# Entering the third block by halves of the sequence: four columns on half 0 ahead of the norms of half 1

## What is computed

```python
h = h + odd_mixer(...)                 # (attn * silu(z)) @ w_out + b_out: the "output product"
h = rms_norm(h, final_norm_g)          # end of the second block
y = rmsnorm(h, norm_w)                 # start of the third block
proj = y @ w_in                        # columns: S5 u, S5 z, SSD z, conv input (x, B, C), dt
xbc = silu(causal_depthwise_conv_3(conv input, width 4))
dt = softplus(dt + dt_bias); A = -exp(A_log)
# SSD over chunks of 128, in four groups of heads, then its gate and norm; S5 and the output products after it
```

## Time and profile before

| | us |
|---|---|
| median of 3 runs (3431.41 to 3432.23) | 3431.87 |
| the profiled execution, own time | 3430.53 |
| its span on the core | 3428.7 |
| TensorE busy | 3157.4 (92%) |
| VectorE busy | 1670.7 (49%) |
| ScalarE busy | 1118.2 (33%) |
| GpSimd busy | 952.0 (28%) |
| share of TensorE in the chain that ended last | 80% |
| mean granted TensorE clock | 0.961 |

### The profile page before, as it was taken

The page is one execution under the profiler, slowest core; times in us unless marked ns, Lnnn a source line. Parts: engine busy times, 40 slices in busy tenths (PEclk is TensorE's granted clock), DMA queues, the critical chain, the costliest instruction groups (busy, mean ns, idle before and its releaser), DMA issues.

```text
span 3428.7 us, 38027 instructions
## 1 busy us (share of the span) xinstructions
PE 3157.4 (92%) x15348; PEld 2474.4 (72%) x15348; DVE 1670.7 (49%) x2730; ACT 1118.2 (33%) x1900; POOL 952.0 (28%) x699
## 2 busy tenths in 40 slices
PE   8999989999999999999999788599887788889998
PEld 6776667767788887778877556477665677778876
DVE  6979541012646543232424675377675234443425
ACT  2126451112521111133411754334343222232334
POOL 4210001113247772145212113011110122253422
PEclk9999999999999999999999899799998999999999
DMA  4110001113323332133311013211111233253222
GB/s 125 43 37 13 13 19 42 48 40 136 110 60 91 93 100 65 43 129 117 97 37 43 25 50 111 76 32 33 41 37 31 56 89 98 83 180 117 86 79 100
DMA packets 251055, 242.22 MB, mean 71 GB/s; under 512 B 15360, under 2 KB 198016, under 8 KB 249856
## 3 DMA queue, kind: packets, MB, share of 16 engines
q1 hardware_dynamic: 228944, 195.52, 18.8%
q10 hardware_dynamic: 21936, 44.27, 3.7%
HBM read 201.03 MB, written 38.73 MB: 70 GB/s over the span
## 4 chain that ended last, share of the span: by engine, by line
PE 80%; DVE 9%; ACT 5%; issue 2%; POOL 2%; DMA 1%; SPq 0%; ACTq 0%; DVEq 0%
PE psum L523 21%; PE psum L524 21%; PE psum L525 21%; PE psum L529 3%; PE psum L641 3%; PE psum L713 1%; PE psum L687 1%; DMA arena<-in_w_in 1%; PE psum L823 1%; PE psum L1116 1%; DVE arena L2783 1%; PE psum L1068 1%; POOL WS L2947 1%; PE psum L1067 1%; DVE arena L2567 1%
## 5 line engine op out<-in xcount | busy, mean ns | idle before, releaser
L2947 POOL TENSOR_TENSOR WS<-arena,WS 128x1024 fp32r<-128x1024 f32 x271 | 670.2, 2477 | 2008.5 <-ACT WS L1132 2008.1
L523 PE MATMUL psum<-XH,WS 128*128 128x512 f32 x2464 | 990.4, 402 | 27.4 <-POOL XL L3003 16.2
L524 PE MATMUL psum<-XL,WS 128*128 128x512 f32 x2464 | 968.4, 393 | 0.0
L525 PE MATMUL psum<-XH,WS 128*128 128x512 f32 x2464 | 967.8, 393 | 0.0
L523 PEld LDWEIGHTS psum<-XH,WS 128*128 128x128 f32 x2464 | 469.3, 190 | 140.2 <-issue 29.5
L524 PEld LDWEIGHTS psum<-XL,WS 128*128 128x128 f32 x2464 | 469.1, 190 | 98.2 <-issue 4.5
L525 PEld LDWEIGHTS psum<-XH,WS 128*128 128x128 f32 x2464 | 467.7, 190 | 100.0
L1132 ACT ACTIVATE WS<-arena 128x1024 fp32r<-128x1024 f32 x271 | 284.5, 1057 | 701.9 <-PE psum L525 243.8
L523 PE MATMUL psum<-WS,XH 128*128 128x512 f32 (+1 forms) x1024 | 396.3, 387 | 19.7 <-DVE XL L2005 7.1
L524 PE MATMUL psum<-WS,XH 128*128 128x512 f32 (+1 forms) x1024 | 393.2, 384 | 0.0
L525 PE MATMUL psum<-WS,XL 128*128 128x512 f32 (+1 forms) x1024 | 393.1, 384 | 0.0
(11 more groups left out here) (288 smaller groups left out, 3249.9 us busy)
## 6 DMA issues: line engine op xcount, KB each, us to landing
arena<-in_w_in SPq DMA_DIRECT2D x85, 512.0 KB, 3.9
arena<-in_w_out SPq DMA_DIRECT2D x48, 512.0 KB, 3.3
arena<-in_w_in_even SPq DMA_DIRECT2D x48, 512.0 KB, 4.1
arena<-in_w_out_even SPq DMA_DIRECT2D x32, 512.0 KB, 3.3
h_spill<-arena ACTq DMA_DIRECT2D x24, 512.0 KB, 3.1
arena<-s_table SPq DMA_DIRECT2D x8, 1536.0 KB, 6.8
arena<-in_w_in_odd SPq DMA_DIRECT2D x18, 512.0 KB, 3.8
s_table<-arena SPq DMA_DIRECT2D x32, 256.0 KB, 2.8
```

What stands on the lines that cost most here:

```text
L523: e.matmul(ps, wh, xh, start=start, stop=False)
L524: e.matmul(ps, wh, xl, start=False, stop=False)
L525: return e.matmul(ps, wl, xh, start=False, stop=stop)
L2947: e.tensor_tensor(lo, raw(book.raw_of.get(("w", u), 0), kbs, n), hi.bitcast(F32), SUB).then_inc(*w.up("w_lo", u))
```

## The change

TensorE's new order: product `ch` 0 (banks 0 to 3), two of the four pieces of product `ch` 1 (banks 4 to 7), the turn of half 0 (banks 0 to 3 again), the other two pieces, then `proj_first`: the dt column and the cv columns 0, 1, 2 of group 0 on half 0, the turn of half 1, the same four on half 1; dt's transposes, cv column 3, dt's small products; the first column of group 1 in both halves, and only then the chunks of group 0, woven as before with what is left.

On ACT the norms of half 1 are woven with these columns, two steps of `od_post(1)` and one copy out of PSUM. The Silus of group 0 come together after the last copy. `RAW3` gets two more buffers, in the room of the tiles of group 1, and the dt column is copied to `DTF`, in the room of `DD3`. The issue of ACT's constants and tables follows the turn of half 1. On DVE the additions of product `ch` 1 are woven one by one with the steps of `od_post(1)`; the convolutions of group 0 all come after the turn of half 1. On SP the weights of the five columns are issued ahead of the waits and the tables; POOL follows the same order of weights.

```diff
+        RAW3 += [view(at, 515) for at in (48.0625, 56.0625)]
+        DTF = [x.rearrange("p a b -> p (a b)") for x in DD3]
...
+        FIRST_RAW = [(0, 0), (1, 0), (2, 0), (0, 1), (1, 1), (2, 1), (3, 0), (3, 1)]
+
+        def ssd_order(prep, chunks, gate):
             for g in range(4):
                 other = chain(prep(g + 1) if g < 3 else iter(()), gate(g - 1) if g else iter(()))
+                if g == 0:
+                    for _ in range(2):
+                        next(other)
                 weave((chunks(g), 1, True), (other, 2 if g else 1, True))
...
(TensorE)
-            for ch in range(2):
-                run(proj_th("o3_ps", (ch,), w3, 512 * ch, 1, lambda tile: [("o3", ch, tile)], x="odo"))
-            for half in range(2):
-                turn_half("b3", XS3, half)
+            run(proj_th("o3_ps", (0,), w3, 0, 1, lambda tile: [("o3", 0, tile)], x="odo", ring=Banks(free_bank, [0, 1, 2, 3])))
+            o3_late = proj_th("o3_ps", (1,), w3, 512, 1, lambda tile: [("o3", 1, tile)], x="odo",
+                              ring=Banks(free_bank, [4, 5, 6, 7]))
+            for _ in range(2):
+                next(o3_late)
+            turn_half("b3", XS3, 0, Banks(free_bank, [0, 1, 2, 3]))
+            run(o3_late)
...
+            proj_first([(("dt_ps", 0), w3[:, 5008:5136], lambda half: [("dt_c", half)])] + [
+                (("cv_ps", 0, i, 0), w3[:, 3072 + 128 * cb:3200 + 128 * cb], lambda half, i=i: [("cv_raw", 0, i, half)])
+                for i, (cb, _) in enumerate(prep_blocks(0)[:3])], "b3", lambda: turn_half("b3", XS3, 1), 4,
+                Banks(free_bank, range(8)))
+            for half in range(2):
+                bank = take(pbk, ("dt_tp", half), ("dt_add", half))
+                w.wait_ge("dt_c", half)
+                for k in range(4):
+                    t = tp(psum[:, bank, tile_of(k)], DTF[half][:, tile_of(k)])
+                t.then_inc(*w.up("dt_tp", half))
+            run(proj_cm("cv_ps", (0, 3), w3, 3072 + 128 * 12, 1, pbk, lambda _, half: [("cv_raw", 0, 3, half)]))
...
(ACT)
-            weave((chain(proj_th(), proj_th()), 1, True), (od_post(0), 1, True))
+            o3_late = proj_th()
+            weave((chain(proj_th(), (next(o3_late) for _ in range(2))), 1, True), (od_post(0), 1, True))
             turn_half("b3", 0, lambda kb: col("norm_w_3", kb), [])
-            run(od_post(1))
-            turn_half("b3", 1, lambda kb: col("norm_w_3", kb), [])
-            w.wait_ge("h_out", "b3", 7)
-            w.wait_ge("turn", "b3", 7, 1)
+            run(o3_late)
+
+            def turn_late():
+                turn_half("b3", 1, lambda kb: col("norm_w_3", kb), [])
+                load_cst()
+                load_t(0)
...
+            def raw_first(n):
+
+                i, half = FIRST_RAW[n]
+                w.wait_ge("cv_ps", 0, i, 0, half)
+                if n >= 4:
+                    j, other = FIRST_RAW[n - 4]
+                    w.wait_ge("cv_c", 0, j, other)
+                    if other == 0:
+                        w.wait_ge("cv_tail", 0, j)
+                e.activation(RAW3[n % 4][:, 3:515], ps_of("cv_ps", 0, i, 0, half), ACT.Copy).then_inc(
+                    *w.up("cv_raw", 0, i, half))
...
+            def first_blocks():
+
+                yield from proj_first([dt_ev] + [lambda half, i=i: raw_first(i + 3 * half) for i in range(3)], turn_late, 4)
+                dt_steps()
+                for half, _ in enumerate(proj_cm(1)):
+                    raw_first(6 + half)
+                for i in range(4):
+                    conv_silu(0, i)
...
-            load_t(0)
-            ssd_order(dt_gen, prep, chunks, gate)
+            weave((od_post(1), 2, True), (first_blocks(), 1, True))
+            ssd_order(prep, chunks, gate)
...
(DVE)
             run(od_post(0))
-            for ch in range(2):
+            for tile in range(4, 8):
+                o3(0, tile)
+            turn_half("b3", 0, lambda kb: col("norm_w_3", kb))
+
+            def o3_late():
                 for tile in range(4, 8):
-                    o3(ch, tile)
-            turn_half("b3", 0, lambda kb: col("norm_w_3", kb))
-            run(od_post(1))
+                    o3(1, tile)
+                    yield
+            weave((o3_late(), 1, True), (od_post(1), 1, True))
             turn_half("b3", 1, lambda kb: col("norm_w_3", kb))
...
+            for n in range(3):
+                w.wait_ge("h_out", "b3", 3)
+                conv_first(n)
             w.wait_ge("h_out", "b3", 7)
+            for n in range(3, 5):
+                conv_first(n)
+            for half in range(2):
+                dt_add(half)
+            conv_first(5)
...
(SP, and the same two calls on POOL)
+            proj_first()
+            run(proj_cm(1))
             for name in ("turn", "b3", 7, 1), ("h_out", "b3", 7), ("nrm_sq", "b3", 7):
                 w.wait_ge(*name)
...
             load_t(0)
-            ssd_order(dt_gen, prep, lambda g: iter([None] * 9), gate)
+            ssd_order(prep, lambda g: iter([None] * 9), gate)
```

More of the change, by code:

```diff
@@ L616, in proj_first @@
                     key = blocks[i][0] + (half,)
-                    bank = take(pb, key, *blocks[i][2](half))
+                    bank = take(ring, key, *blocks[i][2](half))
                     w.wait_ge("w_lo", u)
@@ L1704, in dt_gen, with dt_steps @@
+            def dt_steps():
                 for half in range(2):
@@ L1731, in prep @@
                     yield from proj_cm(1, raw_ev)
-                    for half in range(2):
-                        w.wait_ge("cv_c", g, i, half)
-                    e.activation(dst, dst, ACT.Silu).then_inc(*w.up("cv_s", g, i))
+                    conv_silu(g, i)
             def before(g, c):
@@ L1791, in scalar_program @@
             w.wait_ge("tb_kst", 7)
-            w.own()
-            load_t(0)
-            ssd_order(dt_gen, prep, chunks, gate)
+            weave((od_post(1), 2, True), (first_blocks(), 1, True))
+            ssd_order(prep, chunks, gate)
             def uproj(e_):
@@ new lines, in conv_first @@
+            def conv_first(n):
+                i, half = FIRST_RAW[n]
+                conv(0, i, half, RAW3[n % 4], RAW3[FIRST_RAW.index((i, 0)) % 4])
+            for n in range(3):
+                w.wait_ge("h_out", "b3", 3)
+                conv_first(n)
+            w.wait_ge("h_out", "b3", 7)
+            for n in range(3, 5):
+                conv_first(n)
+            for half in range(2):
+                dt_add(half)
+            conv_first(5)
+            w.wait_ge("dt_ln")
+            e.scalar_tensor_tensor(DTt, DTt, 0.0, AA, MAX, A_).then_inc(*w.up("dt_v", 0))
@@ new lines, in vector_program @@
+            w.wait_ge("dt_al")
+            w.own()
+            e.scalar_tensor_tensor(AA, DTt, -1.0, alog.rearrange("p (u h) -> p u h", u=1).broadcast_to([128, 8, 16]),
+                                   M, M).then_inc(*w.up("dt_v", 1, also=[("dt_aa",)]))
+            for n in range(6, 8):
+                conv_first(n)
+            acs, bank = ACS.rearrange("p a b -> p (a b)"), book.bank("dt_acs")
+            w.wait_ge("dt_acs")
+            e.tensor_copy(acs, psum[:, bank, 0:128]).then_inc(*w.up("dt_v", 2))
@@ L2705, in before @@
+            w.own()
+            e.scalar_tensor_tensor(DEC.rearrange("p a b -> p (a b)"), acs, -1.0, psum[:, bank, 128:256], M,
+                                   A_).then_inc(*w.up("dt_v", 3, also=[("dt_dec_in",)]))
+            def prep(g):
+                for i in range(4):
+                    yield from proj_cm(1, lambda _, half: conv(g, i, half, RAW3[half], RAW3[0]))
             def before(g, c):
```

148 lines of the change are left out of this document (58 added, 90 removed).

## The result

| | before | after |
|---|---|---|
| median, us | 3431.99 | 3375.27 (3375.03 to 3377.49, 4 runs) |
| profiled execution, own time | 3430.53 | 3375.43 |
| its span | 3428.7 | 3373.6 |
| TensorE busy | 3157.4 | 3143.3 |

The ratio is 0.984 with an interval of 0.9824 to 0.9855, a gain of 56.7 us where 43.2 was forecast.

A forecast was written before the change was run, and what follows sets the result against it. The entry stretch was taken as bound by latencies, its surroundings by TensorE. A gain of 48.7 less a loss of 5.5 in the first group's chunks gave 43.2, so 3431.87 should become 3388.7 us, range 3379 to 3401.

The forecast's parts named there:

- margin of 2 us: Turn of half 1: last normed tile ready near 20 us after the last product, TensorE's four half columns last 21.8.
- Rival A: Entry: norms of half 1 late after all, 3 to 6 us of wait and 2 of clock, 3396; chance 0.18.
- B: First group's chunks: they give more back, 14 us instead of 5.5, 3397; chance 0.14.
- D: Slower than before: longer unbroken matmuls bring the granted clock from 2.4 to 1.2 GHz, 3445; chance 0.03.
- E: Entry: an in-order ACT or DVE wait lets only the split pieces move, near 3424 to 3431; chance 0.03.
- C: Entry and chunks: all new waits hidden, gain 51.2 and little loss in the chunks, 3381; chance 0.10.
- The turns: Turns of both halves: about 3.5 us each, plus 1.5 for half 0, and 0.5 and 0.5 for half 1.
- The first group's chunks: First chunk to the second group's first chunk: a loss of 5.5 us, bounds 0 and 14.
- +2.1 for a late second chunk: First group: pulled-ahead column's Silu before the first Exp puts the second chunk 11.5 us after the first, not 9.4.
- +2.4 for two bare steps less the Silu wait: First group's end: two chunk steps without columns, +2.6 and +4.2, against the 4.4 us Silu wait that goes.
- The wait of 4.4 for the last Silu goes: Wait ahead of the second group's first chunk disappears, credited as 4.4 us against the chunks' loss.
- Nothing there is in the diff: Everything later than 2343 us is unchanged; the prediction fails as a whole if something there grows.

The follow-up runs named there:

- at3: Kernel after with the turn of half 1 after three columns of half 0 instead of four; 3389.35 us, ratio 0.9887.
- spread: Kernel after with the steps beside the chunks laid out for all four groups; 3368.13 us, ratio 0.9822.
- best: Kernel after, own first group, two middle groups' steps laid out, one step a chunk in the last group; 3365.33 us, ratio 0.9809.
- The second measurement: The changed kernel as it is, run again beside the kernel before; 3380.48 us, ratio 0.9861.
- turn_only: Kernel before with only the turn of half 0 inside the last product and the additions woven with the norms of half 1; 3422.27 us, ratio 0.9986.
- d16_before: Kernel before with 16 extra transposes in the second chunk front of the second group; 3429.70 us.
- d16_after: Kernel after with 16 extra transposes in the second chunk front of the second group; 3383.37 us.
- d32_after: Kernel after with 32 extra transposes in the second front of the second group's first chunk; 3381.52 us.

## Why the prediction was wrong

**Right: what binds, and what replaces it.** The stretch was bound by latencies, and the change took them out. The last normed tile came at T + 20.2 (forecast 20), TensorE wanted it at T + 21.8 (21.8), and the margin of 2 us was 1.6; at3 shows that with half a column less it is a wait. The last convolution ended 37.5 us after the second halves began (38) and the Silus 39.7 after (40). The first chunk came at 2224.9 (2227), the second group's at 2295.8 (2299). The granted clock was 1.00 in the stretch (above 0.93). Rival A (late norms), B (chunks that give 14 us back), D (a clock that falls without idle) and E (nothing but the split pieces) are all refuted by the waits above. C, all new waits hidden, was the nearest with 3381, and even it was 5.7 us too late. One figure in D is off: 43 us are about a thirtieth of the 1286 us behind 2143, not a fiftieth; nothing rests on it.

**The turns, 1.1 us.** I took 5.0 and 4.5 us for them, and they took 4.55 and 3.88: the stops for four banks and for the fourth column's bank are 0.25 us each. The Trainium skill (TensorE: Matmul & The Clock Gate, Part 4: PE-mode transpose) would have transposes run without the full clock; here 28 of them took 3.28 us amid a stretch with a granted clock of 1.00, while 32 took 5.52 us in at3, after 2.75 us of idle, and even there the clock rose during the turn. It is the idle time ahead that shows in these rows, not the kind of instruction.

**The first group's chunks, 1.4 us.** I had +2.1 for a late second chunk, +2.4 for two bare steps less the Silu wait, and +1 for the clock. From the moments of the chunks: the second came after 8.98 us, where it was 9.37 in the earlier trace rows, -0.4; the third came after 10.35 where it was 8.62, +1.7, with no idle, but at the lower level for part of it, right behind the wait of 1.92:

```profile
2233.83:2244.18 10.35, 10.35 (x55) 8.51 (x56) 7.60 (x15) 5.18 (x8) 2.36 (x1) 0.84 0.19 52
```

The last two steps took 16.35 us where they had been 24.68 with 10.88 of columns, +2.55; the rest +0.2. So the bare steps were sized well, and what failed is the term of 2.1, by the order on ScalarE. Its timeline around the first two chunks:

```profile
2226.17 0.60 ACT L1786 ACTIVATE arena<-psum 128x512 f32<-128x512 f32 x1 [0.52 <-PE psum L981]
...
2232.56 1.28 ACT L1747 ACT_TABLE_LOAD   x1
2233.85 1.06 ACT L1747 ACTIVATE arena<-arena 128x1024 f32<-128x1024 f32 x1
...
2236.36 1.28 ACT L1786 ACT_TABLE_LOAD   x1
2237.65 0.60 ACT L1786 ACTIVATE arena<-psum 128x512 f32<-128x512 f32 x1
```

I had the Silu of the pulled-ahead column, with its table loads, in front of the first chunk's Exp (L1786). It comes behind it, in front of the second chunk's Exp. So the second chunk waited only for VectorE, which had both convolutions of that column to do, and the Silu held up nothing on TensorE: the third chunk came without a wait. The Trainium skill (ScalarE: Activation LUTs, What ACT_TABLE_LOAD costs) counts a drain besides the load for each switch, which by an estimate would have made that chain 2.8 us longer. The load at 2232.56 took the 1.28 us that the Trainium skill gives for it in the same place, but the Silu began 0.01 us after it, and no drain shows in these rows.

**A wait was priced at its idle time alone, 2.7 us.** This is the first step that failed. "The wait of 4.4 for the last Silu goes" counted 4.4 us. In the kernel before the chunk behind that wait took 15.18 us, TensorE busy throughout; in the kernel after, the same chunk without a wait right ahead of it (the last, of 1.26 us, ends 1.7 us before) took 12.46:

```profile
2342.96:2358.14 15.18, 15.18 (x62) 12.92 (x62) 5.95 (x13) 4.09 (x6) 2.39 (x1) 0.81 0.13 36
```
```profile
2295.83:2308.29 12.46, 12.46 (x64) 10.56 (x63) 7.60 (x20) 2.94 (x5) 2.40 (x1) 1.00 0.15 43
```

Granted clock 0.81 against 1.00 for the same matmuls. The wait of 4.4 was worth 7.1. The six executions that keep the wait have 14.8 to 15.2 us there; the seven with no wait there and the order of the kernel after have 12.5. In the entry stretch I had counted this (9.3 us of the 51.2), since there I worked from the stretch's length; here I worked from the wait.

**"Nothing there is in the diff", 6.7 us.** This is the second and the larger step. I took everything outside the entry as fixed to a fraction of a microsecond. It isn't: 5.3 us came behind it and 1.4 ahead of it, from equal instructions, with 16.2 us less at the lower level behind it and 3.4 us less ahead of it. By all runs the part behind, where its instructions are the same, lies between 1065.3 and 1070.6 us, and the origin between 2103.1 (spread) and 2109.1 (best). The 5.3 us come with the new order and came again; the place of the origin changes from one execution to the next. The range had no room for either: from the uncertainty of the entry alone it reached 9.7 us down, and two parts that each move by 5 us needed as much again. Without these 6.7 us the time would have been 3382.0, inside the range; without the 2.7 alone it would have been 3378.0, still outside. The second measurement, where the gain is 46.4 us (3380.48 against 3426.86), is near the forecast by luck: its entry is the same 204.6 and so is what lies behind, but its origin lies 5.1 us later, and the kernel before was 5.1 us faster beside it.

The last 1.5 us: I had set the median 1.3 us above the profiled execution, as it was before; after the change both agree.

## What to carry to other kernels

Price a wait of the bounding engine by the length of the stretch around it, idle time and slow matmuls together: here 4.4 us of idle were worth 7.1, and 2.75 us cost 4.4. Before crediting a change with microseconds far from it, cut both traces at common moments: 6.7 of 55.1 us lay where nothing was changed, and equal code took 1065.3 to 1070.6 us. And when work is moved ahead of a stage, look at the end of the stage for steps that now stand bare; spreading two lists of steps over the chunks, without touching the entry, gained 18.3 us. What it moved across a group's border cost 7.3 us in the next group with one step beside each chunk there, and 0.5 us at most with two.

## What the runs showed of the hardware

That equal instructions take different times with the other engines busy for the same time and with no more idle time on TensorE (305 matmuls in 50.7 us at 0.89 or 54.5 us at 0.86 of the clock) was new to me, and that it repeats: 67.45, 67.45 and 67.47 us in three executions, 70.48 and 70.49 in two others, and values between in turn_only (69.3) and before (70.3). Added work was free once (d16_before), cost about twice its length once (1.8 us of transposes cost 3.4 in d16_after), and about its length once (3.6 us cost 3.4 in d32_after), as the time at the lower level fell by 3.4 us, grew by 3.5 or stayed. The clock also rose from half to full in the middle of a turn, with only transposes running (at3). A trace that shows a difference of 3 us in a stage far from the edit is no sign that the edit removed a wait there.
